# Where a two-block network makes its memory operands: low parts behind the eviction, and key and value blocks spread differently

## The reference, cut to what matters

```python
def second_block(x, mem, mem_norm_gain, norm_gains, ...):
    mem_n = rms_norm_2(mem, mem_norm_gain)          # 256 memory tokens
    for layer in range(2):
        g = norm_gains[layer]
        hn = rms_norm_2(x, g[0])
        y = mlstm_mixer(hn, ...) if layer % 2 == 0 else stick_breaking_mixer(hn, ...)
        x = x + rms_norm_2(y, g[1])
        y = memory_cross_attention(rms_norm_2(x, g[2]), mem_n, w_q[layer], w_kv[layer], w_o[layer])
        x = x + rms_norm_2(y, g[3])
        y = swiglu_ffn(rms_norm_2(x, g[4]), w_gate_up[layer], w_down[layer])
        x = x + rms_norm_2(y, g[5])
    return x

def memory_cross_attention(h, mem_n, w_q, w_kv, w_o):
    q = (h @ w_q).reshape(B, S, 4, 256)
    kv = (mem_n @ w_kv).reshape(B, 256, 2, 4, 256)   # needs nothing of x
    k, v = kv[:, :, 0], kv[:, :, 1]
    p = softmax(einsum(q, k) / 16)
    return (einsum(p, v)).reshape(B, S, 1024) @ w_o
```

## Time and profile before

| | |
|---|---|
| median of 3 runs | 1780.34 us |
| lowest and highest | 1778.22 and 1781.63 us |
| the profiled execution | 1781.91 us, its span 1780.1 us (1.8 us lie around the span) |
| PE busy | 1692.0 us, 95% of the span |
| DVE, ACT, POOL busy | 66%, 53%, 19% |
| one weight block of 512 KB: load, high part, low part | 3.5 us to landing (SP), 0.99 us (ACT), 1.18 us (DVE), means or medians |

### The profile page before, as it was taken

One profiled execution on the slowest core, in us unless ns is written; L12 is line 12 of the kernel. 1 busy time (PEld: TensorE's weight loads), 2 busy tenths in 40 slices (PEclk: granted clock), 3 DMA queues, 4 the chain that ended last, 5 costly groups with the idle time before them and its releaser, 6 DMA issues.

```text
span 1780.1 us, 32609 instructions
## 1 busy us (share of the span) xinstructions
PE 1692.0 (95%) x13172; PEld 1616.0 (91%) x13172; DVE 1174.5 (66%) x1995; ACT 947.7 (53%) x1699; POOL 332.4 (19%) x304
## 2 busy tenths in 40 slices
PE   6999999999999999999988999999979999989997
PEld 6898889999987899999888999999979988889997
DVE  6999886555577745556676655766656746466665
ACT  5677764544455645545555545544455654354443
POOL 0000010243412112334111101002232110010025
PEclk8999999999999999999999999999999999999999
DMA  5433334555532345555334434555543443335653
GB/s 178 131 119 108 118 107 145 167 175 178 178 94 72 98 135 197 189 184 174 125 116 140 154 118 160 169 183 184 168 146 119 133 129 126 99 122 173 190 180 108
DMA packets 76325, 257.47 MB, mean 145 GB/s; under 512 B 8464, under 2 KB 12560, under 8 KB 75920
## 3 DMA queue, kind: packets, MB, share of 16 engines
q1 hardware_dynamic: 76176, 255.39, 44.8%
HBM read 254.31 MB, written 1.05 MB: 143 GB/s over the span
## 4 chain that ended last, share of the span: by engine, by line
PE 73%; DVE 12%; ACT 7%; issue 6%; POOL 2%; DMA 0%; POOLq 0%; DVEq 0%; SPq 0%; ACTq 0%
PE pb L140 72%; DVE WL L159 3%; DVE TMP L171 2%; DVE SCR L171 2%; POOL SCR L159 2%; ACT SCR L149 2%; ACT L156 1%; DVE SCR L159 1%; ACT WH L149 1%; PE pb L143 1%; DVE HNL L171 1%; ACT ASH L149 1%; ACT TMP L149 1%; ACT Rbuf L149 1%; ACT SCR L150 0%
## 5 line engine op out<-in xcount | busy, mean ns | idle before, releaser
L140 PE MATMUL pb<-HNH,WH 128*128 128x256 f32 (+1 forms) x2120 | 613.5, 289 | 6.9 <-DVE WL L159 2.7
L159 DVE TENSOR_TENSOR WL<-RAW,WH 128x1024 fp32r<-128x1024 f32 (+4 forms) x514 | 605.3, 1179 | 12.7 <-ACT WH L149 12.2
L140 PE MATMUL pb<-HNH,WL 128*128 128x256 f32 (+1 forms) x2120 | 602.3, 284 | 0.0
L140 PE MATMUL pb<-HNL,WH 128*128 128x256 f32 (+1 forms) x2120 | 602.3, 284 | 0.0
L149 ACT ACTIVATE WH<-RAW 128x1024 fp32r<-128x1024 f32 (+4 forms) x514 | 507.2, 989 | 150.0 <-PE pb L140 144.8
L140 PE MATMUL pb<-ASH,WH 128*128 128x256 f32 (+1 forms) x1560 | 457.6, 293 | 15.9 <-DVE WL L159 10.9
L140 PE MATMUL pb<-ASH,WL 128*128 128x256 f32 (+1 forms) x1560 | 448.9, 288 | 0.0
L140 PE MATMUL pb<-ASL,WH 128*128 128x256 f32 (+1 forms) x1560 | 448.3, 287 | 0.0
L140 PEld LDWEIGHTS pb<-HNH,WH 128*128 128x128 f32 x2120 | 401.7, 189 | 14.9 <-issue 7.9
L140 PEld LDWEIGHTS pb<-HNH,WL 128*128 128x128 f32 x2120 | 401.9, 190 | 0.0
L140 PEld LDWEIGHTS pb<-HNL,WH 128*128 128x128 f32 x2120 | 400.2, 189 | 1.1
(11 more groups left out here) (146 smaller groups left out, 1662.3 us busy)
## 6 DMA issues: line engine op xcount, KB each, us to landing
RAW<-in_w_gu SPq DMA_DIRECT2D x88, 512.0 KB, 4.1
RAW<-in_w_up SPq DMA_DIRECT2D x64, 512.0 KB, 3.5
RAW<-in_w_down SPq DMA_DIRECT2D x64, 512.0 KB, 3.5
RAW<-in_w_ssd SPq DMA_DIRECT2D x48, 512.0 KB, 3.5
RAW<-in_w_xkv SPq DMA_DIRECT2D x32, 512.0 KB, 3.5
RAW<-in_w_mlin SPq DMA_DIRECT2D x24, 512.0 KB, 3.5
RAW<-in_w_fd SPq DMA_DIRECT2D x32, 384.0 KB, 3.0
RAW<-in_w_sbqkv SPq DMA_DIRECT2D x24, 512.0 KB, 3.6
```

Of the source, the lines that this page charges most:

```text
L140: return self.eng.matmul(o, l, r, start=start, stop=stop, skip_group_check=skip) if self.eng else Nothing()
L159: return self.eng.tensor_tensor(o, a, b, op) if self.eng else Nothing()
```

## The change

Two things are moved; no instruction is added or dropped.

1. In `dve_ffn`, in the last down quarter of layer 0, `dve_mem(q, "mem2", m)` stands behind the eviction of the same step m.
2. The fills of the memory's keys and values: layer 0's key blocks 5 and 6 go from behind `mlo` to steps 3 to 6 of mLSTM's drain, which now has a key block at every step 0 to 6; behind `mlo` stand key block 7 and value head 0 first (3 weight blocks instead of 2), then value heads 1 and 2 at m = 0 and 2; the cross-attention drain keeps value head 3 alone, at step 9. Layer 1's value head 2 goes from behind `sbo` to step 26 of the stick-breaking drain; behind `sbo` only head 3 is left, ahead of the sum.

```diff
-    p += xkv[0][0:5] + out("mlo", xkv[0][5:12])
-    p += [("xq0", 0, m) for m in range(8)] + xkv[0][12:16] + out("xo0", xkv[1][0:5])
+    p += xkv[0][0:7] + out("mlo", xkv[0][7:14])
+    p += [("xq0", 0, m) for m in range(8)] + xkv[0][14:16] + out("xo0", xkv[1][0:5])
-    p += [("sbqkv", 0, m) for m in range(24)] + xkv[1][10:12] + out("sbo", xkv[1][12:16])
+    p += [("sbqkv", 0, m) for m in range(24)] + xkv[1][10:14] + out("sbo", xkv[1][14:16])
...
-        FILL = {"mlo": [("k", 0, 5), ("k", 0, 6), ("k", 0, 7), ("v", 0, 0), ("v", 0, 1)],
+        FILL = {"mlo": [("k", 0, 7), ("v", 0, 0), ("v", 0, 1), ("v", 0, 2)],
...
-                "sbo": [("v", 1, 2), ("v", 1, 3)], "xo1": [], "fd1": []}
+                "sbo": [("v", 1, 3)], "xo1": [], "fd1": []}
...
-        ML_FILL = [0, 1, 2, 4, 5]
...
             for m in range(7):
-                if m in ML_FILL:
-                    pe_fill(q, "k", 0, ML_FILL.index(m))
+                pe_fill(q, "k", 0, m)
...
         def xa_fill(l, n):
-            return [("v", 0, n - 6)] if l == 0 and n in (8, 9) else []
+            return [("v", 0, 3)] if l == 0 and n == 9 else []
...
                         i, b = dve_block(q, fd_name(l, q4), q4 % 2, m, T2)
-                        if l == 0 and q4 == 3:
-                            dve_mem(q, "mem2", m)
                         q.wait_ge(*use[i])
...
                             q.tt(TMP[:, 6 + x % 2, 0:T2], b, R, ALU.mult).then_inc(*evd(i))
+                        if l == 0 and q4 == 3:
+                            dve_mem(q, "mem2", m)
...
             for n in range(24, 28):
-                if n == 24:
-                    pe_fill(q, "v", 1, 1)
+                if n in (24, 26):
+                    pe_fill(q, "v", 1, n // 2 - 11)
```

More of the change, by code:

```diff
@@ L2092, in act_mlstm @@
             for m in range(7):
-                if m in ML_FILL:
-                    act_fill(q, "k", 0, ML_FILL.index(m))
+                act_fill(q, "k", 0, m)
                 for h, k in ml_cores(24 + m):
@@ L2210, in dve_mlstm @@
             for m in range(7):
-                if m in ML_FILL:
-                    dve_fill(q, "k", 0, ML_FILL.index(m))
+                dve_fill(q, "k", 0, m)
                 for h, k in ml_cores(24 + m):
@@ L2613, in act_sb @@
             for n in range(24, 28):
-                if n == 24:
-                    act_fill(q, "v", 1, 1)
+                if n in (24, 26):
+                    act_fill(q, "v", 1, n // 2 - 11)
                 for c, k in sb_cores(n):
@@ L2665, in dve_sb @@
             for n in range(24, 28):
-                if n == 24:
-                    dve_fill(q, "v", 1, 1)
+                if n in (24, 26):
+                    dve_fill(q, "v", 1, n // 2 - 11)
                 for c, k in sb_cores(n):
```

## The result

The changed kernel takes 1763.53 us, the median of four runs (1761.6 to 1765.78); the kernel before takes 1779.28 beside it (1777.54 to 1781.63). The ratio is 0.9911, 95% interval 0.9891 to 0.9932: 15.75 us less, where 14.2 were forecast. The profiled execution is the 1765.78 one, with a span of 1764.0 us.

The account below looks back on a forecast made before the run. PE is busy 95% of the span, so only its idle and lower-clock time can shrink. Terms -7.3 (part 1), -3.8 (parts 2 to 4) and -3.1 (5 and 6) sum to -14.2 us: median 1766.2 us, range 1760 to 1773.

Parts of the forecast that it names:

- part 1: Layer 0's last down quarter: low part behind the eviction opens the 3.5 us loop; gain 7.3 us, bounds 5 to 10.3.
- parts 2: mLSTM's drain: two more key blocks cover PE's waits; drain 1.5 us later, 1.6 back by the clock, net -0.1 us.
- 3: Behind mlo: later chain start and last value head at m = 2 cost +2.1 us, from +1 to +4.
- part 6: Behind sbo: nothing between sum and next product; -2.4 us for the moved value head, -1.3 us for the clock.
- two-step loop: Last down quarter after the edit: the loop spans two steps, 4.25 us for two, 2.1 us a step without disturbance.
- walk of the eight steps: Last down quarter: POOL held until DVE's run ends, DVE held while POOL runs; 2.4 us a step, last eviction at 1307.4.
- Part 4: Cross-attention drain: value head 2's blocks leave and the long softmax wait stays covered; -5.8 us.
- Part 5: Stick-breaking drain: a value head fills the 3.43 us wait, output product starts later; +0.6 us, 0 to +2.
- The clock's share: Behind sbo: less work run at PE's lower clock; -1.3 us, with 0 as the other end.
- A: Last down quarter: POOL and DVE contention costs nothing, 2.1 us a step, -10.3 us there, 1763 in all; chance 0.10.
- B: Last down quarter: the chain through ACT's square replaces the loop, 3 us or less gained there, 1775 in all; chance 0.15.
- C: Filled drains: the weight ring starves, 16 output blocks each wait 1.1 us for loads, 1784 in all; chance 0.04.

Follow-up runs that it names:

- e5: Changed kernel with ACT's square of step m-1 behind the memory's high part of step m, in layer 0's last down quarter: 1763.44 us, ratio 0.9905.
- e4: Changed kernel with DVE's low parts in layer 0's last down quarter reading a PSUM bank in place of SBUF (numbers wrong, sizes kept): 1761.42 us, ratio 0.9902.
- e3: Kernel before with only layer 1's value head 2 moved into the stick-breaking drain: 1775.94 us, ratio 0.9983.
- e6: Changed kernel with ACT's eviction of the last value head behind mlo moved behind the norm's sixth step: 1766.06 us, ratio 0.992.
- e1: Kernel before with only the low part of mem2 moved behind the eviction in layer 0's last down quarter: 1766.59 us, ratio 0.9941.
- e7: Changed kernel with layer 1's value head 3 behind the sum at sbo (m = 0), not ahead of it: 1761.1 us, ratio 0.9889.
- e8: Changed kernel with one fill ahead of the sum behind mlo instead of two, value heads at m = 0, 2 and 4: 1761.17 us, ratio 0.9894.
- e11: Changed kernel, unaltered, run once more: 1766.15 us, ratio 0.9924.
- e2: Kernel before with only layer 0's key and value blocks moved as in the change: 1777.18 us, ratio 0.9987.

## Why the prediction was right, point by point

The traces give -16.4 us for the stretches touched, where -14.2 were forecast. Most of the 2.2 us is part 1; parts 2 and 3 missed by 0.4 us the other way, and part 6 by 0.2 the same way. Both sums hold some 3 us of clock, behind mLSTM's drain and behind sbo, and one pair of traces can't show that they are the change's. The times alone leave a gain of 12 to 19 us (ratio 0.9891 to 0.9932), so it is partly luck that 15.75 came so near.

**Part 1: right in kind, too small: -9.65 for -7.3 us.** The two-step loop is there, two steps of 2.16 us in which DVE waits for the chain only once; e5 showed that POOL and DVE alone are nearly as slow, 2.12 us a step. The step that was mis-sized is the walk of the eight steps "with POOL held until DVE's run is over". In the trace POOL is not held for the whole run: at 1290.70 its addition asks while ASL runs, gets in when ASL ends (0.93 us in all), and it is DVE's split that then waits, 1.35 us in place of 0.81. POOL's addition, and the chain behind it, so come sooner than by my order, and each step loses less. The pace is 2.25 and not 2.4: 1.1 us over seven steps. From the last eviction to the end of the sum it is 1307.60 - 1301.72 = 5.9 us and not 6.8, as PE waits 0.68 us for the last pair and 0.23 us for the last ASL where I had 2.4 and 1: another 0.9. The last 0.4 us are where I read the ends: the first eviction comes 0.2 us earlier than the shift of the landmarks, and the stretch is counted to the start of the logarithm, 1321.80 before, where the forecast counted to the end of the sum's products, 1321.5 (in the changed kernel the two are 0.04 us apart). The Trainium skill, "SBUF — State Buffer", section "Who interferes with whom", has the later instruction blocked until the first is done; the trace agrees, 1.35 us for the split that comes behind the addition and 0.81 for the one that comes first, and e4 measured what it does to the time here, 1.41 us. My error was in who comes later, not in the rule.

**Part 2: right, -0.1 for a measured +0.15.** The drain ended 1.68 us later (1.5 forecast), the 102 matmuls behind took 12.05 us in place of 13.6, a gain of 1.53 (1.6 forecast). The second number is in part luck: it rests on what the trace of before happened to show, and e3 had it without the cover.

**Part 3: right, +2.3 for +2.1.** By the stretches it is mlo and xa0 together less part 2. From the eviction to the product it took 4.34 us for the 4.58 of the forecast, +1.9; another 0.4 lies where the forecast had none, from that product to the next logarithm (4.94 us against 4.52). e6 showed the cause of most of it, 2.04 us.

**Part 4: right, -5.80 for -5.8**, and no wait took the place of the fill. Parts 2 to 4 are -3.36 for -3.8; the 0.4 us are in parts 2 and 3.

**Part 5: right, +0.55 for +0.6**, with one PE wait of 0.55 us left in the drain.

**Part 6: -3.94 for -3.7.** From logarithm to product it took 9.18 for 9.49 us. The clock's share was forecast as 1.3; e1's trace has -1.50 in xa1 with sbo as it was, which leaves 2.44 for the value head that moved (2.4 forecast), the same 2.44 that e7 gave back. So the clock's share is not the change's for sure. All traces together speak for a share, without proving it: with the changed kernel's order behind sbo (after, e3 to e6, e8, e11) xa1 is -3.6 to -3.9 in all seven, with the order of before (before, e1, e2) it is 0, -1.50 and -0.35. So the new order lay within 0.35 us in every execution seen, and the old one lost up to 1.5 us in some.

**Rivals.** A gave 10.3 us for a quarter without contention; e4 has 11.06, so its arithmetic held to 0.8 us and its condition did not: contention costs 1.4 us. B fell: the pair's wait for ACT's square lies in the two-step loop and does not add to it. C fell: no load and no split is waited for in a filled drain, and the dense stretch is as before:

```profile
1124.00:1184.00 60.00, 60.00 (x510) 60.00 (x509) 42.18 (x66) 29.06 (x44) 0.00 (x0) 1.00 0.58 179
```

**What stays open.** The clock steps in unchanged code, mostly 1.1 to 1.6 us each, and up to 5.4 us in the MLA stage: they come in different places from one execution to the next, and no experiment here moved them on purpose.

## What to carry to other kernels

An eviction that frees the bank of the next block should stand ahead of side work that waits for another engine; behind it, the wait for that engine closes a loop of one step, and turning the two round makes it a loop of two. Work to fill a norm's wait is worth most behind its sum, even where its splits and evictions lengthen the chain (2.4 us here for 5.3 covered), and evictions that nobody waits for belong behind the chain's own steps. Price such a move by finding the same order elsewhere in the trace: the norm waits of parts 3 and 6 and the drain of part 4 were read off a twin place and came within 0.3 us, part 1 had to be walked and missed by 2.4 us.

## What the runs showed of the hardware

- When a POOL and a DVE instruction exclude each other, the loser is whichever asks second, for each instruction anew: POOL gets in between two DVE instructions that follow each other in the queue. The split then takes 1.35 us and POOL's addition 0.93; without two SBUF inputs on DVE it is 0.81 and 0.74 side by side.
- A wait of 2.7 us on PE is followed by the lower clock in some executions and not in others of the same code (e1 and e3 behind mLSTM's drain: 0.91 and 1.00 over 20 us), worth 1.5 us there. The changed kernel's times range from 1761.6 to 1768.22 us; its two traces differ by clock steps alone, everything else agrees to 0.04 us.
